# Down projection by seven half-size products of split operands

## The reference, cut to what matters

```
u = h @ w_up                                   # (1024, 5632)
u = _conv_grid_3x3(u, conv_w, conv_b)
a, v = jnp.split(u, 2, axis=-1)
y = (jax.nn.silu(a) * v) @ w_down              # (1024, 2816) @ (2816, 1024)
x = x + gate2 * y                              # gated residual add
out = x * lax.rsqrt(jnp.mean(x * x, axis=-1, keepdims=True) + 1e-6) * final_norm
```

## Time and profile before

| | |
|---|---|
| median of 3 runs | 1649.36 us (1646.6, 1649.36, 1652.43) |
| profiled execution, span from first to last instruction | 1648.8 us |
| PE busy | 1605.8 us (97%) |
| DVE busy | 1228.9 us (75%) |
| ACT busy | 560.9 us (34%) |
| POOL busy | 450.6 us (27%) |
| mean granted TensorE clock | 0.989 of full speed |

### The profile page before, as it was taken

The page is one execution under the profiler, slowest core; times in us unless marked ns, Lnnn a source line. Parts: engine busy times, 40 slices in busy tenths (PEclk is TensorE's granted clock), DMA queues, the critical chain, the costliest instruction groups (busy, mean ns, idle before and its releaser), DMA issues.

```text
span 1648.8 us, 20721 instructions
## 1 busy us (share of the span) xinstructions
PE 1605.8 (97%) x8142; PEld 1197.5 (73%) x8142; DVE 1228.9 (75%) x1761; ACT 560.9 (34%) x892; POOL 450.6 (27%) x435
## 2 busy tenths in 40 slices
PE   7999999999999989999999999999999999999997
PEld 2545555995599955656588888888888887887886
DVE  5587887699766679888876599889888898434435
ACT  2544343552343322222744322222222223223332
POOL 5001101221233256565134433233333333100000
PEclk9999999999999999999999999999999999999999
DMA  9276454864398540000523211111111112522332
GB/s 348 82 263 222 132 192 166 255 159 108 105 292 232 167 153 26 14 26 14 205 96 122 65 51 52 51 50 40 52 51 51 45 46 85 196 90 89 115 130 88
DMA packets 201389, 194.79 MB, mean 118 GB/s; under 512 B 40117, under 2 KB 155135, under 8 KB 201164
## 3 DMA queue, kind: packets, MB, share of 16 engines
q1 hardware_dynamic: 194608, 190.00, 36.1%
q10 hardware_dynamic: 6396, 3.20, 0.7%
q0 software_dynamic: 288, 0.27, 0.1%
HBM read 151.32 MB, written 42.12 MB: 117 GB/s over the span
## 4 chain that ended last, share of the span: by engine, by line
PE 56%; DVE 5%; ACT 1%; issue 1%; POOL 1%; DMA 0%; ACTq 0%; DVEq 0%; POOLq 0%
PE PS L2159 10%; PE PS L2163 10%; PE PS L2161 10%; PE PS L2198 5%; PE PS L2200 5%; PE PS L2202 5%; PE PS L2017 4%; PE PS L2032 2%; DVE Qbd L2460 2%; PE PS L2119 1%; PE PS L2121 1%; PE PS L2120 1%; PE PS L2054 1%; DVE AT L2476 1%; DVE Ex L2441 1%
## 5 line engine op out<-in xcount | busy, mean ns | idle before, releaser
L2631 DVE SCALAR_TENSOR_TENSOR acc<-PS,fcol,acc 128x945 f32<-128x945 f32 (+2 forms) x176 | 215.1, 1222 | 29.2 <-ACT acc L2290 23.6
L2631 DVE SCALAR_TENSOR_TENSOR act<-PS,fcol,act 128x945 f32<-128x945 f32 (+2 forms) x176 | 215.1, 1222 | 21.7 <-ACT act L2290 16.2
L2159 PE MATMUL PS<-h2hi,whi 128*128 128x512 f32 x704 | 219.5, 389 | 0.0
L2161 PE MATMUL PS<-h2lo,whi 128*128 128x512 f32 x704 | 219.3, 389 | 0.0
L2163 PE MATMUL PS<-h2hi,wlo 128*128 128x512 f32 x704 | 219.3, 389 | 0.0
L425 PE MATMUL PS<-hT,wq 128*128 128x512 f32 (+1 forms) x432 | 163.1, 537 | 0.0
L1969 POOL TENSOR_TENSOR wlo<-wu,whi 128x1024 fp32r<-128x1024 f32 x44 | 106.4, 2422 | 207.3 <-ACT whi L2283 206.9
L2161 PEld LDWEIGHTS PS<-h2lo,whi 128*128 128x128 f32 x704 | 132.1, 188 | 27.4
L2163 PEld LDWEIGHTS PS<-h2hi,wlo 128*128 128x128 f32 x704 | 132.1, 188 | 27.4
L2159 PEld LDWEIGHTS PS<-h2hi,whi 128*128 128x128 f32 x704 | 132.1, 188 | 27.4
L2642 DVE TENSOR_TENSOR wrlo<-wr,wrhi 128x1024 fp32r<-128x1024 f32 x41 | 50.2, 1224 | 128.4 <-ACT wrhi L2380 128.4
(11 more groups left out here) (314 smaller groups left out, 2858.7 us busy)
## 6 DMA issues: line engine op xcount, KB each, us to landing
wm<-in_w_mod_dram SPq DMA_DIRECT2D x24, 1024.0 KB, 7.7
wu<-in_w_up_dram SPq DMA_DIRECT2D x44, 512.0 KB, 3.8
wr<-in_w_down_dram SPq DMA_DIRECT2D x44, 512.0 KB, 3.4
wq<-in_w_in_dram SPq DMA_DIRECT2D x12, 512.0 KB, 9.0
gdn_x_image<-ztile SPq DMA_DIRECT2D x10, 516.0 KB, 9.9
gdn_xt_image<-ztile SPq DMA_DIRECT2D x10, 516.0 KB, 8.1
GR<-gdn_gc_rows SPq DMA_DIRECT2D x20, 256.0 KB, 4.9
gdn_w_image<-Wm SPq DMA_DIRECT2D x20, 256.0 KB, 4.6
```

The costliest lines, as they stand in the source:

```text
L2159: pe.matmul(PS[:, b + half, :], whi[k][u][:, kk, :], h2hi[:, 4 * half:4 * half + 4, kk, :], start=(kk == 0), stop=False)
L2161: pe.matmul(PS[:, b + half, :], whi[k][u][:, kk, :], h2lo[:, 4 * half:4 * half + 4, kk, :], start=False, stop=False)
L2631: tp = v.scalar_tensor_tensor(out=t_[:, r0:r1, c0:c1], in0=up[:, r0 + dr:r1 + dr, c0 + dc:c1 + dc], scalar=tap_col(j, k, f), in1=t_[:, r0: ...
```

## The change

The product is cut in halves in all three dimensions. A is the activations by tokens, B is `w_down`: A11 is tokens 0 to 511 of features 0 to 1407, A12 the same tokens of the other features, A21 and A22 the other tokens; B12 is the right 512 columns of the upper 1408 rows, and so on. Eight products of halves would be the full product; Winograd's form of Strassen's scheme needs seven, each of 11 steps (`KH`), and sums of blocks:

S1 = A21 + A22, S2 = S1 - A11, S3 = A22 - S2, S4 = A12 - S2; T3 = B22 - B12, T2 = B11 + T3, T1 = B12 - B11, T4 = B21 - B11 - T3. The products in order: A11 B11, S2 T2, A12 B21, S3 T3, S1 T1, A22 T4, S4 B22.

- A step is now 12 matmuls of the same shape (4 token tiles, one bank each, three split terms). Products alternate between banks 0 to 3 and 4 to 7. The first product is copied by ACT to `y10`; the partial sums Y00, Y01, Y10 and Y11 (128 x 4 x 512 each) are kept in SBUF.
- `NB7` stays 4; a slot's weights are 128 x 512. `HEAD7` is 6, `TAIL7` is 4.
- POOL makes S1, S2, S4 and S3 in place of the activations or into `as7`, T1 and T4 in the slot's `raw7`, gates and adds the residual (quarters `xq`) to the Y blocks. DVE makes T3 and T2, reads the banks, and keeps the low parts from step 6.
- The squares are summed in two halves per token tile; the stores are 128 x 512, 16 of them, all after the last step's loads.

```diff
-        STEPS7 = 2 * FT
-        TAIL7 = 3
-        HEAD7 = 3
+        NR7 = 3
+        KH = FT // 2
+        PRODUCTS7 = ("A11 B11", "S2 T2", "A12 B21", "S3 T3", "S1 T1", "A22 T4", "S4 B22")
+        STEPS7 = len(PRODUCTS7) * KH
+        TAIL7 = 4
+        HEAD7 = 6
```

On SP:

```diff
+                def t3_in(j):
+                    second(j, b_block(0, 1, j))
+                    sp.dma_start(t3[j][:, :], b_block(1, 1, j)).then_inc(s_7y[j % NR7], 16)
+
+                def step_in(s):
+                    p, j, u = at7(s)
+                    if p == 1 and j + NR7 < KH:
+                        t3_in(j + NR7)
+                    if p in (4, 5):
+                        second((p - 3) * KH + j, b_block(0, 0, j))
+                    if p == 3:
+                        return
+                    if s >= NB7:
+                        sp.wait_ge(s_7f, s - NB7 + 1)
+                    k, c = ((0, 0), (0, 0), (1, 0), None, (0, 1), (1, 0), (1, 1))[p]
+                    sp.dma_start(raw7[u][:, :], b_block(k, c, j)).then_inc(s_7w[u], 16)
...
+                for s in range(NB7, STEPS7):
+                    if s == 8:
+                        for j in range(NR7):
+                            t3_in(j)
...
+                    step_in(s)
```

On POOL:

```diff
+                def sums_of_a(j):
+                    g.wait_ge(s_6g, KH + j + 1)
+                    g.tensor_tensor(tok_half(j, 1), tok_half(j, 1), tok_half(KH + j, 1), ALU.add).then_inc(s_7s, 1)
...
+                    g.tensor_tensor(tok_half(j, 0), tok_half(j, 1), tok_half(j, 0), ALU.subtract).then_inc(s_7s, 1)
...
+                def s4_of(j):
+                    g.wait_ge(s_7lv, 2 * KH + j - HEAD7 + 1)
+                    g.wait_ge(s_7s, 2 * j + 2)
+                    g.tensor_tensor(tok_half(KH + j, 0), tok_half(KH + j, 0), tok_half(j, 0), ALU.subtract).then_inc(s_7s, 1)
...
+                for s in range(HEAD7):
+                    low7(s)
                 gated(FT - 1)
+                for j in range(KH):
+                    sums_of_a(j)
+                for j in range(KH):
+                    s4_of(j)
+                for j in range(KH):
+                    s3_of(j)
+                    if 3 <= j < 3 + TT:
+                        gate_and_add(y01, 1, j - 3, 1, 1, 0)
+                for j in range(KH):
+                    t1_of(j)
+                    if 6 <= j < 6 + TT:
+                        gate_and_add(y10, 0, j - 6, 3, 2, Y01_DONE)
+                for j in range(KH):
+                    t4_of(j)
```

On PE:

```diff
+                    pe.matmul(PS[:, b, :], ahi7[u][:, tok], rhi7[u][:, :], start=fresh, stop=False, skip_group_check=True)
+                    pe.matmul(PS[:, b, :], ahi7[u][:, tok], rlo7[u][:, :], start=False, stop=False, skip_group_check=True)
+                    return pe.matmul(PS[:, b, :], alo7[u][:, tok], rhi7[u][:, :], start=False, stop=(j == KH - 1), skip_group_check=True)
```

On DVE:

```diff
+                def t3_of(j):
+                    v.wait_ge(s_7y[j % NR7], second_loads7(j))
+                    v.tensor_tensor(t3[j][:, :], t3[j][:, :], r2[j % NR7][:, :], ALU.subtract).then_inc(s_7t3, 1)
...
+                for s in range(HEAD7, KH):
+                    low7(s)
+                    if s >= KH - NR7:
+                        t3_of(s - KH + NR7)
+                t2_of(0)
+                for j in range(KH):
+                    if j + NR7 < KH:
+                        t3_of(j + NR7)
+                    if j + 1 < KH:
+                        t2_of(j + 1)
+                    low7(KH + j)
...
+                    if s == 6 * KH + 5:
...
+                        v.tensor_tensor(m7[:, :, :], PS[:, TT:2 * TT, :], gate_row(0), ALU.mult).then_inc(s_7m, 1)
...
+                        v.tensor_tensor(y10[:, :, :], y10[:, :, :], m7[:, :, :], ALU.add).then_inc(s_7e, 1)
...
+                for t in range(TT, NL):
+                    rstd(t, t - TT + 1)
+                    finish(t, 0, y10)
+                    finish(t, 1, y11)
                 for t in range(TT):
+                    second_half(t)
+                    if t:
+                        rstd(t - 1, TT + t)
+                        finish(t - 1, 1, y01)
```

More of the change, by code:

```diff
@@ L1780, in program @@
-        s_7w = [sem(f"w_down_row_in{i}") for i in range(NB7)]
+        KH = FT // 2
[3 more added lines that the diff above has]
+        HEAD7 = 6
+        STEP_AT = (175, 183, 15, 23)
+        raw7 = [place(f"raw7{i}", [P, HALF], STEP_AT[i]) for i in range(NB7)]
+        rlo7 = [place(f"rlo7{i}", [P, HALF], STEP_AT[i], F32R) for i in range(NB7)]
+        rhi7 = [place(f"rhi7{i}", [P, HALF], STEP_AT[i] + 2, F32R) for i in range(NB7)]
@@ new lines, in program @@
+        y10, y01, y11, y00 = [place(f"y7{n}", [P, TT, HALF], 143 + 8 * i) for i, n in enumerate(("10", "01", "11", "00"))]
+        m7 = place("m7", [P, TT, HALF], 63)
+        fng = place("fng", [P, D], 71)
+        sqj = [place(f"sqj{i}", [P, HALF], 75 + 2 * i) for i in range(2)]
+        fsa = place("fsa", [P, NL], 207)
+        fsb = place("fsb", [P, NL], 207.0625)
+        fea = place("fea", [P, NL], 207.125)
+        frt = place("frt", [P, NL], 207.1875)
+        frs = place("frs", [P, NL], 207.25)
@@ L1898, in store @@
-                def store(t):
-                    sp.wait_ge(s_7o, t + 1)
-                    sp.dma_start(out[0][t * P:(t + 1) * P, :], x1b[:, t, :]).then_inc(s_out, 16)
-                for i in range(NB7, STEPS7):
-                    if i - NB7 == FT - 1:
-                        sp.wait_ge(s_7b[TT - 1], 1)
-                    else:
-                        sp.wait_ge(s_7f, i - NB7 + (1 if i - NB7 < FT else 0))
-                    row(i)
-                    if i >= FT + 10 and i < FT + 10 + TT:
-                        store(i - FT - 10)
@@ new lines, in store @@
+                def store(t, c, y):
+                    sp.dma_start(out[0][t * P:(t + 1) * P, c * HALF:(c + 1) * HALF], y[:, t % TT, :]).then_inc(s_out, 16)
+                for t in range(TT, NL):
+                    sp.wait_ge(s_7o, 2 * (t - TT) + 1)
+                    store(t, 0, y10)
+                    sp.wait_ge(s_7o, 2 * (t - TT) + 2)
+                    store(t, 1, y11)
+                for t in range(TT):
+                    sp.wait_ge(s_7o2, t + 1)
+                    store(t, 0, y00)
+                    sp.wait_ge(s_7o, 2 * TT + t + 1)
+                    store(t, 1, y01)
@@ new lines, in banks_free @@
+                def banks_free(p, t):
+                    if p < 2:
+                        pe.wait_ge(s_6v[t // 2], FT - 1 + p)
+                    elif p == 2:
+                        pe.wait_ge(s_7p1, 1)
+                    else:
+                        pe.wait_ge(s_7q, p - 2)
+                for s in range(STEPS7 - TAIL7):
+                    p, j, u = at7(s)
+                    ready(s)
+                    for t in range(TT):
+                        if j == 0:
+                            banks_free(p, t)
+                        mm = part(s, t)
+                    mm.then_inc(s_7f, 1)
+                    if j == KH - 1:
+                        pe.sem_inc(s_7p, 1)
@@ L2223, in _ @@
+                for s in range(STEPS7 - TAIL7, STEPS7):
+                    ready(s)
                 for t in range(TT):
-                    for i in range(STEPS7 - TAIL7, STEPS7):
-                        mm = part(i, t)
+                    for s in range(STEPS7 - TAIL7, STEPS7):
+                        mm = part(s, t)
                     mm.then_inc(s_7b[t], 1)
```

373 lines of the change are left out of this document (243 added, 130 removed).

## The result

| | before | after |
|---|---|---|
| median | 1650.13 us (4 runs, 1646.6 to 1652.43) | 1674.8 us (4 runs, 1670.69 to 1675.43) |
| profiled span | 1648.8 us | 1673.7 us |
| PE busy | 1605.8 us | 1593.4 us |
| DVE busy | 1228.9 us | 1339.9 us |
| POOL busy | 450.6 us | 623.6 us |

The account below looks back on a forecast made before the run. TensorE was taken as the bound: 29.9 us of matmuls go, 36.3 us of waits come, the last four steps start at 1627.6, the end adds 22.7 (1650.3), clock 1.6: 1652 against 1648.8, range 1628 to 1674.

Parts of the forecast that it names:

- The matmuls removed: Down projection on TensorE: 924 matmuls at the same 0.2267 us each, 132 fewer, -29.9 us.
- The mechanism: DVE's lows and POOL's SBUF-reading operations alternate one to one; a met DVE operation costs 1.57 us, otherwise 0.60.
- The second rival: DVE-POOL meetings cost both operations whole, 1.83 us in place of 1.57, giving 1667; chance 0.29.
- First two products: DVE's queue of 17 met operations up to step 12's first low delays PE by +16.4 us.
- Third: Third product: one POOL operation per step falls in DVE's idle time, costing 0.
- Fourth: Fourth product: four steps of 4.37 us, 6.6 behind, about 5 covered by the slots' slack: +1.7.
- Sixth: Sixth product: T4's POOL operations meet two lows, 3.14 us per step, plus one reading of banks: +5.5.
- Seventh with the tail: Gating and adding Y10 ahead of step 72's lows, +1.8; unhidden load, copy and lows before the closing group, +4.9.
- Loads and clock: Stage's 256 KB loads take 2.8 us; step 8's weights land about 1414.4; clock falls after long waits add 1.6.
- the first rival: DVE and POOL hardly meet; only waits at steps 2 and 8, the tail and end remain: 1621; chance 0.27.
- The end: Squares, roots, scalings and store take +22.7 us from the last four steps' start; 11.8 lie behind PE.
- The case that I held likeliest: Engines take turns at 1.57 us per met DVE operation: 1652, own range 1642 to 1660, chance 0.44.

Follow-up runs that it names:

- writes only: Changed kernel with each of POOL's 109 block sums and gatings replaced by two memsets of the same block, so POOL reads nothing; 1636.66 us, ratio 0.9917.
- an idle POOL: Changed kernel with POOL's 109 operations left out and only their signals given, the fourth product taking A22 for S3; 1636.43 us, ratio 0.9911.
- The run without the last load: Changed kernel without the last of four residual loads (1 MB), quarter Y11 getting the residual already there; 1674.51 us, ratio 1.0137.
- the last version: Seven products, S1 on POOL in the up projection, other sums and gating on DVE, changed loads and Y order, three-step tail, reordered end; 1625.98 us, ratio 0.9849.
- the tail group of three steps: Changed kernel with TAIL7 = 3 in place of 4, so three steps in the closing group; 1677.21 us, ratio 1.0154.
- S1 early: Changed kernel with POOL making the eleven S1 sums during the up projection, not in products 1 and 2; 1666.07 us, ratio 1.0087.

## Why the prediction was right or wrong

**The matmuls removed: right.** 924 matmuls at 0.2267; the stage began at 1392.59, 0.25 before the forecast.

**The mechanism: right. Its price, and where it was charged: too low.** The forecast was that DVE's lows meet POOL one to one; the trace shows it, and writes only or an idle POOL take it away. I had charged 1.57 for a met operation; it is 1.69. The 0.97 in it was 1.40, a *pitch* of the earlier trace rows, less a *duration* of 0.42 (0.98 by the numbers), and I added it to a *pitch* of 0.60. But keeping to one measure does not mend it. DVE of before, just ahead of the meeting in the earlier trace rows:

```profile
345.48 0.42 DVE L1521 TENSOR_TENSOR blk<-co,so 128x256 f32<-128x256 f32 x1
345.94 0.42 DVE L1524 TENSOR_TENSOR so<-so,blk 128x256 f32<-128x256 f32 x1
```

Its pitch is 0.46, so by pitches the price there is 0.94, and a met operation here would be 1.54; by durations it is 1.37 - 0.42 = 0.95, and 0.68 + 0.95 = 1.63 for the 1.76 seen. Those rows hold two meetings, of operations half as wide; what makes the price 1.09 here no run shows. The second rival had put the point from which it decides at 1.62, and priced 1.83: the truth lies between. The rule of the Trainium skill's "SBUF — State Buffer", section "Who interferes with whom", holds in its first half, that the two exclude each other; read as one whole operation behind the other, pitch added to pitch, it gives 1.83, and the 1.69 decides against that reading. By itself the price is the smaller part of the error, 17 x 0.12 = 2.0 in the first two products and 2.6 in the sixth; the larger parts are meetings charged nowhere (product 7), slack credited that was not there (product 4), and loads and clock. By product:

- First two products, forecast +16.4: 21.4 lost. 17 x 1.69 = 28.7 for the charged 26.7, and the queue began late: step 8's weights were asked for at 1411.44, behind four loads (1 MB) asked for from 1409.65 on, and landed at 1416.6 in place of 1414.4.
- Third, 0: seen +2.5 from step 12 to step 36 with no wait over 0.4, most of it at the low clock after 1446.64 (the stretch 1440 to 1450 has 0.68).
- Fourth, +1.7: 4.6, as steps of 3.40 (2 x 1.70) followed one another and the slots' slack covered less than the 5 us credited.
- Fifth, +6.0: 8.8. Sixth, +5.5: 8.3, of which 11 x 2 x 0.12 = 2.6 are the price alone.
- Seventh with the tail, +1.8 and +4.9 (and 1.6 of clock): 13.6. Step 72 waited 5.01 for the 1.8 forecast. The run without the last load shows that it is not that load (0.4 of the time from step 66 to 72) but that I let eight Y11 operations pass beside the lows at no price. The tail's wait, 4.79, is as forecast.

**Loads and clock: too low.** The kernel without meetings loses 17.2 to 19.2 at the tail group, where the first rival had 7.2: the wait at step 8 is 3.1 and more, not 1.3, and the clock fell more often than I charged: 0.70, 0.81 and 0.68 in the three stretches from 1420 to 1450, after the waits of 3.08 and 7.01, and 0.72 from 1640 to 1650, after 5.01. Nor does the length of a wait alone tell: in the last version the clock stays at 1.00 (1425 to 1430) after the wait of 2.11, and is 0.63 (1604 to 1608) after that of 2.10, where I had set the fall between 1.88 and 2.27. So of the 21.3 us by which the loss was underrated (59.2 for 37.9), 8.4 are this (17.2 for 7.2 + 1.6), and 12.9 the meetings with the chains through POOL (42.0, that is 59.2 - 17.2, for 29.1). That split rests on the kernel with POOL idle, which has no chain through POOL; by the one with writes, which has, it is 10.4 and 10.9.

**The end: right, but for PE's part.** 23.3 from the tail group's start for 22.7, set by squares, roots and scalings, as the tail group of three steps shows. PE's last matmul ends 13.1 after that start, not 10.9 (the clock is 0.54 from 1650 to 1655), so 10.2 lie behind it and not 11.8.

1392.59 + 198.6 + 59.2 + 23.3 = 1673.7, the span. The case that I held likeliest named the right mechanism, but its own range ended at 1660. The median of 1674.8 is 0.8 above the whole range, which ended at 1674, and the profiled span of 1673.7 just inside it; both are nearest to the second rival. The direction, slower, had the largest of the three chances, 0.40. Of the signs that I had named, the long POOL operations (1.6 to 1.7), the lows over 1 us, the wait of over 5 at step 11 (7.01), the third product without waits and the wait of about 4.9 before the last group came; the over 11 us behind PE did not.

## What to carry to other kernels

Moving elementwise work to GpSimd beside a VectorE that reads two SBUF operands doesn't add an engine: the trace here shows both doing their operations nearly one after the other (1.69 a pair, for 0.60 and 1.25 alone), so add up their times. Count such work on VectorE itself, and put on GpSimd what falls where VectorE reads PSUM or waits, as S1 early does. When a price is read off a trace, keep to one measure, and look for rows of the width at hand: two meetings of half-wide operations gave 0.94, and the ones here cost 1.09.

## What the runs showed of the hardware

- GpSimd's memsets (0.52 us for 128x512) go beside VectorE's two-operand operations at no price to these: pitch 0.60 with and without.
- Cutting GpSimd's operations from 512 to 256 columns halves the price of a meeting (1.09 to 0.54 us), and the two engines keep strictly to turns; alone, 256 columns start every 0.69 us, 512 every 1.25.
- A 256 KB load of weights took 2.6 us in the median (part 6 of the profile's page), 2.8 in the forecast; where 1 MB was asked for less than 2 us ahead, 5.2.
- Two waits of TensorE of one length, 2.11 and 2.10 us in the last version, were followed by a granted clock of 1.00 and of 0.63.
